# One hybrid decoder block on one core: block keys moved through DRAM scratch, gate projection from raw x in column groups, scores and probabilities half a unit later

## The chip, the cores and the metric

The kernel runs on one core of a Trainium2 chip. The metric is the device time of one execution in microseconds, as the median of several executions of the same program. A profiled execution gives the trace that is read here.

## What is computed

A sequence of 256 tokens with a width of 1024 goes through one decoder block, all in float32: an RMS norm, an input projection, a mixer with two groups of heads, an output projection, a SwiGLU feed-forward layer and a final norm.

```python
h = rms_norm(x, norm1_gain[l])
proj = h @ w_in[l]
gq, gk, gv, gr, g_low, mq, mk, mv = parts            # 256, 256, 512, 512, 16, 512, 512, 512 columns
log_a = log_sigmoid(g_low @ w_gate_up[l] + b_gate[l]) / 16
o_gla = rms_norm(gla_chunked(gq, gk, gv, log_a)) * silu(gr)
q_m, k_m = rotary(mq, positions), rotary(mk, positions)
o_moba = rms_norm(moba_attention(q_m, k_m, mv))       # 256 tokens are one block: causal softmax attention
x = x + concatenate([o_gla, o_moba]) @ w_out[l]
h = rms_norm(x, norm2_gain[l])
x = x + (silu(h @ w_ffn_gate[l]) * (h @ w_ffn_up[l])) @ w_ffn_down[l]
return rms_norm(x, final_norm_gain)
```

## The kernel before

All matrix products with weights are made from three float32r products: each operand is split into a high part (a rounded copy) and a low part (the rest), and hi x hi, hi x lo and lo x hi are added up in PSUM (`product`, L505 to L510). Attention, transposes and the small products take plain float32 operands, each of which shows in the trace as two matmul records.

The weights come in **units** of 128 x 2048 floats (1 MB). SyncE (SP) loads a unit with two DMAs into one of three raw buffers (`rows_unit`, L344; the DMAs have line L342), ScalarE (ACT) rounds it to `w_hi` (L877), VectorE (DVE) subtracts to get `w_lo` (L1137), and TensorE (PE) runs 24 matmuls of 512 columns over it (`in_unit`, L593). `w_hi` and `w_lo` have six buffers. Units 0 to 11 are the input projection, two for each block of 512 columns, in the order gate queries and keys, block queries (`mq`), block keys (`mk`), block values, gate values, `gr`; units 12 to 15 are the output projection; then eleven feed-forward phases follow with three units each. The load of unit u waits until the `lo` part of unit u - 3 is made (`raw_free`, L362).

Units 0 and 1 are special: they are loaded, split and multiplied row by row (128 x 512 pieces, `load_first` L330, `split_first` L903 and L1150, `first_row` L555) beside the transposes of x (L534) and the scaling of the transposed x by the norm gain (`take_xT`, L897 on ACT for the high part, L1144 on DVE for the low part).

The order of work on every engine is written out by hand, and each engine works in that order. SP is one queue of DMA issues too: what stands behind a wait there is issued late. On PE the small products stand between the two token halves of a unit (`midway`) or behind a unit (`after`):

```python
            midway = {2: [logits], 7: [moba_k_transposed], 8: [moba_scores],
                      9: [probs_transposed], 10: [moba_outputs, gla_updates], 11: [gla_outputs, lambda: heads_transposed(0, (3, 0))]}
            after = {3: [cumulate], 7: [gla_scores]}
```

What the change touches:

- `gate_low` (L580): the 16-column projection `g_low`. ACT copies the weights four times side by side as high part, GpSimd (POOL) makes the low part (L477), and 16 float32r matmuls of 256 columns (L589, L590) multiply them with the split, gain-scaled x.
- `rotate` (L1228) on DVE: rotary for `mq` (which 0) and `mk` (which 1), six operations each.
- The queries of the block attention are turned by one DVE transpose within 32 x 32 squares (L1257), written to DRAM (`squares_out`, L387) and read back as columns by four DMAs (`columns_back`, L392); ACT copies them to `mT_q` (L964). The keys are turned by PE (`moba_k_transposed`, L635) in the middle of unit 7 and copied out of PSUM by ACT (L960) and DVE (L1261) to `mT_k`.
- `moba_scores` (L654) in the middle of unit 8, the softmax on DVE (L1276 to L1286) and ACT (L973), `probs_transposed` (L670) in the middle of unit 9.
- Behind it: the squares of the heads on ACT (L986, L1007), their sums on DVE (L1298), the low part of the transposed heads (`take_headsT`, L1326, through L1141), and the output projection on PE, which starts when that low part is there.

## Time and profile before

| | |
|---|---|
| median of 3 executions | 302.33 us (301.77 to 302.42) |
| the profiled execution's own time | 301.75 us |
| its span in the trace | 300.0 us |
| PE busy | 292.4 us (97%), 1373 matmul records |
| DVE busy | 242.4 us (81%) |
| ACT busy | 171.6 us (57%) |
| POOL busy | 19.1 us (6%) |
| DMA | 55.45 MB, mean 185 GB/s |
| chain that ended last | PE 94%, DMA 2%, DVE 1%, issue 1%, POOL 1% |
| mean granted TensorE clock | 0.996 of full speed |

The busy time is the union of the instructions of an engine. The chain that ended last is followed back from the last instruction: at each step to what released it, or to the instruction before it on its engine. The own time of the execution is 1.75 us longer than its span.

### The profile page before, as it was taken

The page shows a single profiled execution, that of the slowest core. Times are in us where ns is not written, and L with a number is a line of the kernel's source. Part 1 is how long each engine was busy: PE and PEld are TensorE (multiplying, and loading weights), DVE is VectorE, ACT ScalarE, POOL GpSimd, SP SyncE. Part 2 cuts the span into 40 slices and gives each one's busy share as a digit, 9 for nine tenths or more (in the row PEclk, how much of TensorE's full clock was granted, in tenths as well). Part 3 has the DMA queues.
Part 4 walks back from the last instruction along what each step waited for, and adds up shares of the span by engine and source line. Part 5 has one row for each costly group of instructions (what it writes and reads, how often), then busy time and mean ns, then how long its engine had stood idle before and what let it go on. Part 6 is the DMA issues. An engine that isn't in the chain of part 4 may idle for free.

```text
span 300.0 us, 4026 instructions
## 1 busy us (share of the span) xinstructions
PE 292.4 (97%) x1373; PEld 243.3 (81%) x1373; DVE 242.4 (81%) x403; ACT 171.6 (57%) x242; POOL 19.1 (6%) x41
## 2 busy tenths in 40 slices
PE   7999999999999999999999999999999999999992
PEld 7788888788898888887888888888888888888881
DVE  1999999977879687988888888889897978787155
ACT  2898999969765897717170808080808080813123
POOL 5050100000021001300000000000000000000011
PEclk9999999999999999999999999999999999999998
DMA  7987836737867121392929292929291929030003
GB/s 235 364 289 266 263 119 251 218 131 264 298 190 227 53 92 70 95 329 90 331 82 336 79 343 69 346 66 352 63 363 47 367 54 366 25 120 0 0 0 140
DMA packets 37318, 55.45 MB, mean 185 GB/s; under 512 B 2950, under 2 KB 26554, under 8 KB 37306
## 3 DMA queue, kind: packets, MB, share of 16 engines
q1 hardware_dynamic: 37140, 55.13, 54.4%
q10 hardware_dynamic: 166, 0.17, 0.2%
q8 instruction: 7, 0.11, 0.2%
q14 instruction: 5, 0.04, 0.0%
HBM read 53.72 MB, written 1.57 MB: 184 GB/s over the span
## 4 chain that ended last, share of the span: by engine, by line
PE 94%; DMA 2%; DVE 1%; issue 1%; POOL 1%; ACT 0%; SPq 0%; POOLq 0%; DVEq 0%
PE acc L508 15%; PE acc L510 15%; PE acc L509 15%; PE aux L508 13%; PE aux L509 13%; PE aux L510 13%; DMA raw<-in_w_in 2%; PE aux L613 1%; PE acc L562 1%; PE acc L565 1%; PE acc L568 1%; PE aux L683 1%; DVE x_sb L1366 1%; PE aux L707 1%; PE aux L665 1%
## 5 line engine op out<-in xcount | busy, mean ns | idle before, releaser
L1137 DVE TENSOR_TENSOR w_lo<-raw,w_hi 128x2048 fp32r<-128x2048 f32 x47 | 105.6, 2286 | 14.5 <-ACT w_hi L877 14.4
L877 ACT CAST w_hi<-raw 128x2048 fp32r<-128x2048 f32 x47 | 87.9, 1908 | 4.4 <-DMA raw<-in_w_ffn_up 2.1
L508 PE MATMUL aux<-w_hi,aT_hi 128*128 128x512 f32 (+1 forms) x180 | 69.8, 388 | 0.0
L509 PE MATMUL aux<-w_lo,aT_hi 128*128 128x512 f32 (+1 forms) x180 | 69.7, 387 | 0.0
L510 PE MATMUL aux<-w_hi,aT_lo 128*128 128x512 f32 (+1 forms) x180 | 69.7, 387 | 0.0
L1432 DVE STREAM_TRANSPOSE reuse_c<-reuse_c 32x128 f32<-32x128 f32 x160 | 48.4, 303 | 2.4
L1080 ACT CAST pT_hi<-reuse_c 128x512 fp32r<-128x512 f32 x10 | 6.2, 621 | 72.9 <-DVE reuse_c L1432 72.9
L508 PE MATMUL acc<-w_hi,aT_hi 128*128 128x512 f32 x118 | 47.1, 399 | 0.0
L510 PE MATMUL acc<-w_hi,aT_lo 128*128 128x512 f32 x118 | 46.1, 390 | 0.0
L509 PE MATMUL acc<-w_lo,aT_hi 128*128 128x512 f32 x118 | 46.0, 390 | 0.0
L508 PEld LDWEIGHTS aux<-w_hi,aT_hi 128*128 128x128 f32 x180 | 33.8, 188 | 6.9
L510 PEld LDWEIGHTS aux<-w_hi,aT_lo 128*128 128x128 f32 x180 | 33.8, 188 | 6.9
L509 PEld LDWEIGHTS aux<-w_lo,aT_hi 128*128 128x128 f32 x180 | 33.8, 188 | 6.8
L508 PE MATMUL acc<-w_hi,pT_hi 128*128 128x512 f32 x80 | 31.3, 392 | 0.0
L510 PE MATMUL acc<-w_hi,pT_lo 128*128 128x512 f32 x80 | 31.2, 390 | 0.0
L509 PE MATMUL acc<-w_lo,pT_hi 128*128 128x512 f32 x80 | 31.2, 389 | 0.0
L510 PEld LDWEIGHTS acc<-w_hi,aT_lo 128*128 128x128 f32 x118 | 22.2, 188 | 4.8
L508 PEld LDWEIGHTS acc<-w_hi,aT_hi 128*128 128x128 f32 x118 | 22.2, 188 | 4.7 <-issue 0.2
L509 PEld LDWEIGHTS acc<-w_lo,aT_hi 128*128 128x128 f32 x118 | 22.2, 188 | 4.4
L1063 ACT ACTIVATE reuse_c<-aux,rstd 128x256 f32<-128x256 f32 x22 | 10.0, 471 | 19.1 <-PE aux L510 17.9
L508 PEld LDWEIGHTS acc<-w_hi,pT_hi 128*128 128x128 f32 x80 | 15.0, 188 | 3.4 <-issue 0.3
L510 PEld LDWEIGHTS acc<-w_hi,pT_lo 128*128 128x128 f32 x80 | 15.0, 188 | 3.2
(203 smaller groups left out, 285.0 us busy)
## 6 DMA issues: line engine op xcount, KB each, us to landing
raw<-in_w_ffn_gate SPq DMA_DIRECT2D x22, 512.0 KB, 4.3
raw<-in_w_ffn_up SPq DMA_DIRECT2D x22, 512.0 KB, 5.4
raw<-in_w_ffn_down SPq DMA_DIRECT2D x22, 512.0 KB, 6.0
raw<-in_w_in SPq DMA_DIRECT2D x20, 512.0 KB, 4.8
raw<-in_w_out SPq DMA_DIRECT2D x8, 512.0 KB, 4.3
raw<-in_w_in SPq DMA_DIRECT2D x8, 256.0 KB, 6.2
x_sb<-in_x SPq DMA_DIRECT2D x2, 512.0 KB, 3.7
m_moves<-reuse_c SPq DMA_DIRECT2D x1, 512.0 KB, 2.7
```

What stands on the lines that cost most here:

```text
L508: nc.tensor.matmul(dst, left_hi[:, k, tok], right_hi, start=first, stop=False)
L509: nc.tensor.matmul(dst, left_hi[:, k, tok], right_lo, start=False, stop=False)
L510: return nc.tensor.matmul(dst, left_lo[:, k, tok], right_hi, start=False, stop=last)
L562: nc.tensor.matmul(acc[:, t, :], aT_hi[:, k, toks[t]], right_hi, start=k == 0, stop=False)
L565: nc.tensor.matmul(acc[:, t, :], aT_hi[:, k, toks[t]], right_lo, start=False, stop=False)
L568: last = nc.tensor.matmul(acc[:, t, :], aT_lo[:, k, toks[t]], right_hi, start=False, stop=k == KC - 1)
L613: last = nc.tensor.transpose(aux[:, bank, n * P:(n + 1) * P], src, ident[:, :])
L877: nc.scalar.copy(w_hi[:, slot % RING, :], raw[:, slot % RAW, :]).then_inc(hi_ready, 1)
L1063: nc.scalar.activation(silu_g[:, t, :], aux[:, GATE_UP_BANKS[parity][t], 0:FF], ACT.Silu, scale=rstd[:, 1, t:t + 1]).then_inc(silu_ready, 1)
L1080: nc.scalar.copy(dst, src.rearrange("p (k s) -> p k s", k=2)).then_inc(hiddenT_hi_ready, 1)
L1137: nc.vector.tensor_tensor(w_lo[:, slot % RING, :], raw[:, slot % RAW, :], w_hi[:, slot % RING, :].bitcast(f32), ALU.subtract).then_inc(lo_ ...
L1432: last = nc.vector.transpose(cols[SQUARE * c:SQUARE * (c + 1), :, :, g, :], rows[SQUARE * g:SQUARE * (g + 1), :, :, c, :])
```

## The change

1. **First loads.** SP issues row 0 of the weights behind the two halves of x, then waits until the first half of x has landed before it issues rows 1 to 7. ACT sums the squares of the first half of x at its start. Unit 2 is split in two halves on ACT and DVE, each when its own DMA has landed, and DVE does it ahead of the casts of the rotary angles.
2. **One table set.** ACT preloads the set with both logarithm and exponential, and the preload between units 5 and 6 is gone.
3. **`gate_low`.** POOL scales the 16 weight columns by the norm gain (two copies side by side, 32 columns), ACT copies the transposed x as it is out of PSUM (four copies of 128 x 512), and PE runs 8 plain float32 matmuls of 256 columns whose left side is 32 columns wide; they go to four groups of 32 output partitions. `w_up` is laid out in four groups (four DMAs for two).
4. **`rotate`.** Five operations for six, the first one of double width, with two temporaries.
5. **Keys.** DVE turns them as it does the queries, after the scratch of the queries has been written (`m_moved_out`), since both use the same squares; SP writes them to DRAM and reads them back by four DMAs, behind the load of unit 11. The eight transposes on PE and the two copies out of PSUM are gone.
6. **Order.** `moba_scores` and `probs_transposed` move from the middle of units 8 and 9 to their end. DVE splits unit 10 ahead of the softmax, not behind it.

```diff
--- before.py
+++ after.py
...
@@ -158,9 +158,10 @@
...
         gate_bias = mv[:, 0, W - QK:W]
-        rot_tmp = mv[:, :, 0:HEADS * HALF].rearrange("p t (h d) -> p t h d", h=HEADS)
-        low_w = w_hi[:, RING - 1, 0:KC * P].rearrange("p (k r w n) -> p k r w n", k=KC, w=2, n=RANK)
+        rot_tmp = [mv[:, :, HEADS * HALF * n:HEADS * HALF * (n + 1)].rearrange("p t (h d) -> p t h d", h=HEADS) for n in range(2)]
+        low_w = reuse_d[:, 512:512 + KC * SQUARE].rearrange("p (k w n) -> p k w n", k=KC, n=RANK)
+        xT_raw = [half[:, :].rearrange("p (b n) -> p b n", b=2)[:, b, :] for half in (reuse_a, reuse_b) for b in range(2)]
...
-        mT_k = reuse_f[:, 1024:2048].rearrange("p (h s) -> p h s", h=HEADS)
+        k_columns = reuse_d[:, :].rearrange("p (c n i) -> p c n i", c=QUADS, i=SQUARE)
+        k_rows = reuse_e[:, 1024:2048].rearrange("p (n c i) -> p c n i", c=QUADS, i=SQUARE)
...
@@ -334,20 +340,22 @@
 
             for t in range(T):
                 sp.dma_start(x_sb[:, t, :], x[0, t * P:(t + 1) * P, :]).then_inc(x_loaded[t], 16)
-            for n in range(KC):
+            load_first(0)
+            sp.wait_ge(x_loaded[0], 16)
+            for n in range(1, KC):
                 load_first(n)
 
...
@@ -367,15 +375,14 @@
                     sp.wait_ge(lo_ready, u - RAW - EARLY + 1)
 
             sp.dma_start(low_raw[:, :, :], w_in[0, :, LOW:LOW + RANK].rearrange("(k p) n -> p k n", p=P)).then_inc(low_loaded, 16)
-            for u in range(EARLY, RAW):
-                rows_unit(u, w_in[0], (u % 2) * 4 * P, 4, BLOCKS[u // 2], 512)
+            rows_unit(EARLY, w_in[0], (EARLY % 2) * 4 * P, 4, BLOCKS[EARLY // 2], 512, half_loaded)
...
             sp.wait_ge(up_zeroed, 1)
-            for n in range(2):
-                sp.dma_start(w_up[n * RANK:(n + 1) * RANK, :], w_gate_up[0]).then_inc(up_loaded, 16)
+            for n in range(QUADS):
+                sp.dma_start(w_up[n * SQUARE:n * SQUARE + RANK, :], w_gate_up[0]).then_inc(up_loaded, 16)
...
@@ -395,7 +402,9 @@
             in_units(RAW, 11)
             squares_out(m_squares_ready, 1, m_moves, m_squares, m_moved_out)
             columns_back(m_moved_out, m_moves, m_columns, m_columns_back)
+            squares_out(k_squares_ready, 1, k_moves, m_squares, k_moved_out)
             in_units(11, IN_UNITS)
+            columns_back(k_moved_out, k_moves, k_columns, k_columns_back)
             for n in range(OUT_UNITS):
                 u = IN_UNITS + n
                 raw_free(u)
@@ -473,9 +482,11 @@
                 nc.gpsimd.tensor_tensor(rstd[:, norm, t:t + 1], ms[:, norm, t:t + 1], minus_half[:, 0:1],
                                         ALU.pow).then_inc(rstd_ready, 1)
 
-            pool.wait_ge(low_hi_ready, 1)
-            nc.gpsimd.tensor_tensor(low_w[:, :, :, 1, :], low_raw[:, :, :].unsqueeze(2).to_broadcast(LOW_COPIES),
-                                    low_w[:, :, :, 0, :].bitcast(f32), ALU.subtract).then_inc(low_lo_ready, 1)
+            pool.wait_ge(low_loaded, 16)
+            pool.wait_ge(gains_ready, 1)
+            nc.gpsimd.tensor_tensor(low_w, low_raw[:, :, :].unsqueeze(2).to_broadcast(LOW_COPIES),
+                                    gains[:, NORM1_ROW:NORM1_ROW + KC].unsqueeze(2).unsqueeze(3).to_broadcast(LOW_COPIES),
+                                    ALU.mult).then_inc(low_w_ready, 1)
...
@@ -580,14 +591,12 @@
             def gate_low():
 
 
-                pe.wait_ge(low_hi_ready, 1)
-                pe.wait_ge(low_lo_ready, 1)
-                pe.wait_ge(xT_hi_ready, KC)
-                pe.wait_ge(xT_lo_ready, KC)
+                pe.wait_ge(low_w_ready, 1)
+                pe.wait_ge(xT_raw_ready, KC // 2)
                 for k in range(KC):
-                    left = w_hi[:, RING - 1, k * P:(k + 1) * P]
-                    nc.tensor.matmul(aux[:, 2, 0:SEQ], left, aT_hi[:, k, :], start=k == 0, stop=False)
-                    last = nc.tensor.matmul(aux[:, 2, 0:SEQ], left, aT_lo[:, k, :], start=False, stop=k == KC - 1)
+                    group = slice(k % QUADS * SQUARE, (k % QUADS + 1) * SQUARE)
+                    last = nc.tensor.matmul(aux[group, 2, 0:SEQ], low_w[:, k, :, :].rearrange("p w n -> p (w n)"),
+                                            xT_raw[k // 2][:, k % 2 * SEQ:(k % 2 + 1) * SEQ], start=k < QUADS, stop=k >= QUADS)
                 last.then_inc(low_in_psum, 1)
...
@@ -631,12 +640,6 @@
                     nc.tensor.matmul(aux[:, 3, dst], tri[:, :], log_hi[:, cols], start=True, stop=False)
                     last = nc.tensor.matmul(aux[:, 3, dst], tri[:, :], log_lo[:, cols], start=False, stop=True)
                 last.then_inc(cum_in_psum, 1)
-            def moba_k_transposed():
-                pe.wait_ge(rotated, 2)
-                for n, bank in enumerate((3, 0)):
-                    transposes(bank, [m_rot[:, 1, t, h, :] for h in (2 * n, 2 * n + 1)
-                                      for t in range(T)]).then_inc(mT_in_psum, 1)
...
@@ -654,16 +657,16 @@
             def moba_scores():
 
                 pe.wait_ge(mT_q_ready, 1)
-                pe.wait_ge(mT_by_act, 1)
-                pe.wait_ge(mT_by_dve, 1)
+                pe.wait_ge(k_columns_back, 16 * QUADS)
                 pe.wait_ge(a_ready, 2)
+                keys = k_columns.rearrange("p g (t h) i -> p t h g i", t=T)
                 for h in range(HEADS):
-                    last = nc.tensor.matmul(aux[:, 1, h * P:(h + 1) * P], mT_q[:, 0, h, :], mT_k[:, h, 0:P],
+                    last = nc.tensor.matmul(aux[:, 1, h * P:(h + 1) * P], mT_q[:, 0, h, :], keys[:, 0, h],
...
                 last.then_inc(scores_in_psum, 1)
                 for h in range(HEADS):
                     last = nc.tensor.matmul(aux[:, 2 + h // 2, (h % 2) * SEQ:(h % 2 + 1) * SEQ], mT_q[:, 1, h, :],
-                                            mT_k[:, h, :], start=True, stop=True)
+                                            keys[:, :, h], start=True, stop=True)
                     if h % 2:
                         last.then_inc(scores_in_psum, 1)
...
@@ -785,9 +788,8 @@
...
-            midway = {2: [logits], 7: [moba_k_transposed], 8: [moba_scores],
-                      9: [probs_transposed], 10: [moba_outputs, gla_updates], 11: [gla_outputs, lambda: heads_transposed(0, (3, 0))]}
-            after = {3: [cumulate], 7: [gla_scores]}
+            midway = {2: [logits], 10: [moba_outputs, gla_updates], 11: [gla_outputs, lambda: heads_transposed(0, (3, 0))]}
+            after = {3: [cumulate], 7: [gla_scores], 8: [moba_scores], 9: [probs_transposed]}
...
@@ -866,7 +868,7 @@
...
-            nc.scalar.preload_act_table(ACT.Exp)
+            nc.scalar.preload_act_table_set("natural_log_exp_and_others")
...
@@ -906,27 +908,36 @@
                 nc.scalar.copy(w_hi[:, n // 4, cols], raw[:, n // 4, cols]).then_inc(first_hi_ready, 1)
...
+            act.wait_ge(x_loaded[0], 16)
+            sum_squares(0, 0)
             act.wait_ge(gains_ready, 1)
             take_xT((0, 1))
+            def copy_xT(pair):
+                act.wait_ge(xT_lo_ready, 2 * pair + 2)
+                nc.scalar.copy(xT_raw[pair], aux[:, pair, :]).then_inc(xT_raw_ready, 1)
             for n in range(1, KC):
                 split_first(n)
                 if n % 2:
                     take_xT((n + 1, n + 2) if n < KC - 1 else ())
-            act.wait_ge(low_loaded, 16)
-            nc.scalar.copy(low_w[:, :, :, 0, :], low_raw[:, :, :].unsqueeze(2).to_broadcast(LOW_COPIES)).then_inc(low_hi_ready, 1)
-            split(2)
-            for t in range(T):
-                sum_squares(0, t)
+                if n in (5, KC - 1):
+                    copy_xT((n - 5) // 2)
+            for h in range(2):
+                act.wait_ge(half_loaded[h], 16)
+                half = slice(h * UNIT // 2, (h + 1) * UNIT // 2)
+                nc.scalar.copy(w_hi[:, EARLY, half], raw[:, EARLY, half]).then_inc((half_hi_ready, hi_ready)[h], 1)
+            for pair in range(2, KC // 2):
+                copy_xT(pair)
+            sum_squares(0, 1)
             split(3)
+            act.wait_ge(low_in_psum, 1)
             take_block(0, gqk)
             split(4)
             act.wait_ge(logits_ready, 1)
             then(nc.scalar.activation(soft, log_a, ACT.Abs))
             then(nc.scalar.activation(soft, soft, ACT.Exp, scale=-1.0))
             nc.scalar.activation(soft, soft, ACT.Ln, bias=one[:, :]).then_inc(soft_ready, 1)
-            act.wait_ge(low_in_psum, 1)
             split(5)
-            nc.scalar.preload_act_table(ACT.Exp)
             split(6)
             act.wait_ge(cum_in_psum, 1)
             nc.scalar.activation(reuse_c[:, 0:512], aux[:, 2, :], ACT.Exp)
@@ -956,8 +967,6 @@
...
             act.wait_ge(rotated, 2)
-            act.wait_ge(mT_in_psum, 1)
-            nc.scalar.copy(mT_k[:, 0:2, :], aux[:, 3, :].rearrange("p (h s) -> p h s", h=2)).then_inc(mT_by_act, 1)
             split(9)
             take_block(3, mv)
...
@@ -1188,15 +1197,21 @@
...
             nearest_turns()
+            for h in range(2):
+                dve.wait_ge((half_hi_ready, hi_ready)[h], 1)
+                half = slice(h * UNIT // 2, (h + 1) * UNIT // 2)
+                last = nc.vector.tensor_tensor(w_lo[:, EARLY, half], raw[:, EARLY, half], w_hi[:, EARLY, half].bitcast(f32),
+                                               ALU.subtract)
+            last.then_inc(lo_ready, 1)
             then(nc.vector.tensor_copy(turns_hi, turns))
             then(nc.vector.tensor_tensor(turns_lo, turns, turns_hi.bitcast(f32), ALU.subtract))
-            split(2)
-            for part in two_pi_parts(5)[:2]:
-                take_off(turns_hi.bitcast(f32), part)
-                take_off(turns_lo, part)
+            take_off(turns_hi.bitcast(f32), two_pi_parts(5)[0])
+            take_off(turns_lo, two_pi_parts(5)[0])
             dve.wait_ge(low_in_psum, 1)
             nc.vector.tensor_copy(lowT[:, :], aux[:, 2, 0:SEQ]).then_inc(lowT_ready, 1)
+            take_off(turns_hi.bitcast(f32), two_pi_parts(5)[1])
+            take_off(turns_lo, two_pi_parts(5)[1])
...
@@ -1232,12 +1247,14 @@
...
-                nc.vector.tensor_tensor(out_a, a, cos, ALU.mult)
-                nc.vector.tensor_tensor(out_b, b, cos, ALU.mult)
-                then(nc.vector.tensor_tensor(rot_tmp, b, sin, ALU.mult))
-                then(nc.vector.tensor_tensor(out_a, out_a, rot_tmp, ALU.subtract))
-                then(nc.vector.tensor_tensor(rot_tmp, a, sin, ALU.mult))
-                nc.vector.tensor_tensor(out_b, out_b, rot_tmp, ALU.add).then_inc(rotated, 1)
+                both, out = (v.rearrange("p t h (w d) -> p t (h w) d", w=2) for v in (m_raw, m_rot[:, which]))
+                nc.vector.tensor_tensor(out, both, cos_t[:, :, :].unsqueeze(2).to_broadcast([P, T, 2 * HEADS, HALF]), ALU.mult)
+                nc.vector.tensor_tensor(rot_tmp[0], b, sin, ALU.mult).then_inc(turned, 1)
+                nc.vector.tensor_tensor(rot_tmp[1], a, sin, ALU.mult).then_inc(turned, 1)
+                dve.wait_ge(turned, 2 * which + 1)
+                nc.vector.tensor_tensor(out_a, out_a, rot_tmp[0], ALU.subtract)
+                dve.wait_ge(turned, 2 * which + 2)
+                nc.vector.tensor_tensor(out_b, out_b, rot_tmp[1], ALU.add).then_inc(rotated, 1)
...
@@ -1256,9 +1273,10 @@
             dve.wait_ge(rotated, 1)
             nc.vector.transpose(m_squares, m_rows).then_inc(m_squares_ready, 1)
             rotate(1)
+            dve.wait_ge(rotated, 2)
+            dve.wait_ge(m_moved_out, 16)
+            nc.vector.transpose(m_squares, k_rows).then_inc(k_squares_ready, 1)
             split(8)
-            dve.wait_ge(mT_in_psum, 2)
-            nc.vector.tensor_copy(mT_k[:, 2:4, :], aux[:, 0, :].rearrange("p (h s) -> p h s", h=2)).then_inc(mT_by_dve, 1)
             split(9)
...
                 last.then_inc(a_ready, 1)
+            split(10)
...
@@ -1285,7 +1304,6 @@
...
-            split(10)
             split(11)
             dve.wait_ge(probT_in_psum, 3)
```

**SP, around unit 11.** Before, the last two blocks of the queue (`reuse_a<-m_moves` reads the queries back):

```order
L387 DMA m_moves<-reuse_c 128x1024 [waits m_squares_ready]
L392 DMA reuse_a<-m_moves 32x4x256 [waits m_moved_out]
L392 DMA reuse_a<-m_moves 32x4x256 x3
L342 DMA raw<-in_w_in 128x2x512 [waits lo_ready]
L342 DMA raw<-in_w_in 128x2x512
L342 DMA raw<-in_w_out 128x1024 [waits lo_ready]
```

And in the changed kernel:

```order
L394 DMA m_moves<-reuse_c 128x1024 [waits m_squares_ready]
L399 DMA reuse_a<-m_moves 32x4x256 [waits m_moved_out]
L399 DMA reuse_a<-m_moves 32x4x256 x3
L394 DMA k_moves<-reuse_c 128x1024 [waits k_squares_ready]
L350 DMA raw<-in_w_in 128x2x512 [waits lo_ready]
L350 DMA raw<-in_w_in 128x2x512
L399 DMA reuse_d<-k_moves 32x4x256 [waits k_moved_out]
L399 DMA reuse_d<-k_moves 32x4x256 x3
L350 DMA raw<-in_w_out 128x1024 [waits lo_ready]
```

Five DMAs for the keys came in, one ahead of the load of unit 11 and four behind it and ahead of unit 12.

**DVE, from the second rotary to the softmax.** Before:

```order
L1240 TENSOR_TENSOR reuse_e<-reuse_e,mv 128x8x64 [waits dve_seq]
L1137 TENSOR_TENSOR w_lo<-raw,w_hi 128x2048 [waits hi_ready]
L1261 COPY reuse_f<-aux 128x512 [waits mT_in_psum]
L1137 TENSOR_TENSOR w_lo<-raw,w_hi 128x2048 [waits hi_ready]
L1270 COPY_PREDICATED reuse_b<-gla_mask,aux 128x2x128 [waits a_in_psum,consts_built,a_zeroed]
...
L1276 TENSOR_TENSOR reuse_e<-aux,causal 128x512 [waits scores_in_psum]
```

And in the changed kernel:

```order
L1257 TENSOR_TENSOR reuse_e<-reuse_e,mv 128x8x64 [waits turned]
L1278 STREAM_TRANSPOSE reuse_c<-reuse_e 128x1024 [waits m_moved_out,rotated]
L1146 TENSOR_TENSOR w_lo<-raw,w_hi 128x2048 [waits hi_ready] x2
L1288 COPY_PREDICATED reuse_b<-gla_mask,aux 128x2x128 [waits a_in_psum,consts_built,a_zeroed]
...
L1146 TENSOR_TENSOR w_lo<-raw,w_hi 128x2048 [waits hi_ready]
L1295 TENSOR_TENSOR reuse_e<-aux,causal 128x512 [waits scores_in_psum]
```

The transpose of the keys stands ahead of the splits of units 8 and 9, the copy out of PSUM between them is gone, and the split of unit 10 stands ahead of the softmax.

## Rows read from the trace of the kernel before

**Rows 1.** The page's part 1: busy time of each engine.
```profile
PE 292.4 (97%) x1373; PEld 243.3 (81%) x1373; DVE 242.4 (81%) x403; ACT 171.6 (57%) x242; POOL 19.1 (6%) x41
```
**Rows 2.** Waits of PE, whole span: us in total, times, longest.
```profile
PE acc L562 <- DVE w_hi L1156: 0.4, 1, 0.4
```
**Rows 3.** The chain that ended last: start us, us, what.
```profile
1.71 5.34 DMA raw<-in_w_in
7.07 0.44 DVE w_hi L1156
7.64 0.70 PE acc L562 x2
...
9.47 0.46 PE acc L562 x2
...
53.08 0.98 PE aux L613 x8
...
56.82 1.09 PE aux L650 x16
...
60.86 0.89 PE aux L661 x8
...
78.44 0.59 PE aux L695 x8
```
**Rows 4.** Timeline of ACT: start us, us, line, operation, idle before.
```profile
6.31 0.84 ACT L900 ACTIVATE aT_hi<-aux,gains 128x256 fp32r<-128x256 f32 x2 [3.04 <-PE aux L534]
8.00 0.62 ACT L906 CAST w_hi<-raw 128x512 fp32r<-128x512 f32 x1 [0.85 <-DMA raw<-in_w_in]
...
15.52 1.91 ACT L877 CAST w_hi<-raw 128x2048 fp32r<-128x2048 f32 x1 [1.07 <-DMA raw<-in_w_in]
...
27.21 1.28 ACT L926 ACT_TABLE_LOAD   x1
...
53.74 0.59 ACT L960 COPY reuse_f<-aux 128x512 f32<-128x512 f32 x1 [0.70 <-PE aux L613]
...
83.37 1.91 ACT L877 CAST w_hi<-raw 128x2048 fp32r<-128x2048 f32 x1 [2.07 <-DMA raw<-in_w_ffn_up]
```
**Rows 5.** Landing times: tile x_sb, then L332 (first rows), then L342 at 40:64.
```profile
DMA to landing us min/median/max: 3.3/3.7/4.2
...
DMA to landing us min/median/max: 5.3/6.2/6.7
...
DMA to landing us min/median/max: 3.4/4.5/6.3
```
**Rows 6.** Timeline of PE.
```profile
18.86 0.28 PE L589 MATMUL aux<-aT_hi,w_hi 128*128 128x256 f32 x1
...
20.86 0.22 PE L577 MATMUL aux<-ident,reuse_d 10*128 10x10 f32 x1
...
90.84 0.39 PE L508 MATMUL acc<-w_hi,aT_hi 128*128 128x512 f32 x1
```
**Rows 7.** Timeline of DVE.
```profile
47.55 1.25 DVE L1257 STREAM_TRANSPOSE reuse_c<-reuse_e 128x1024 f32<-128x1024 f32 x1
...
52.83 2.28 DVE L1137 TENSOR_TENSOR w_lo<-raw,w_hi 128x2048 fp32r<-128x2048 f32 x1
...
88.04 1.22 DVE L1298 TENSOR_REDUCE ss_h<-reuse_c 128x8 f32<-128x1024 f32 x1 [0.74 <-ACT reuse_c L1007]
...
89.38 1.41 DVE L1141 SCALAR_TENSOR_TENSOR aT_lo<-aux,gains,aT_hi 128x512 fp32r<-128x512 f32 x2
```
**Rows 8.** The page's part 6: KB each, median us to landing.
```profile
m_moves<-reuse_c SPq DMA_DIRECT2D x1, 512.0 KB, 2.7
```
**Rows 9.** Timeline of SP's queue: unit 11, unit 16.
```profile
55.58 0.47 SPq L342 DMA_DIRECT2D raw<-in_w_in  x1
...
77.92 0.38 SPq L342 DMA_DIRECT2D raw<-in_w_ffn_gate  x1
```
**Rows 10.** One stretch: us, busy of each engine, PEclk, DMA share, GB/s.
```profile
59.00:60.00 1.00, 1.00 (x6) 0.81 (x5) 0.95 (x3) 1.00 (x1) 0.00 (x0) 1.00 1.18 303
```

More of the change, by code:

```diff
@@ L227, in build_block @@
         gain_f_loaded = sem("gain_f_loaded")
+        half_loaded = [sem(f"half_loaded_{h}") for h in range(2)]
+        half_hi_ready = sem("half_hi_ready")
         raw_loaded = [sem(f"raw_loaded_{s}") for s in range(RAW)]
@@ L336, in _, with load_unit, rows_unit @@
                 sp.dma_start(x_sb[:, t, :], x[0, t * P:(t + 1) * P, :]).then_inc(x_loaded[t], 16)
[L337 removed]
+            load_first(0)
+            sp.wait_ge(x_loaded[0], 16)
+            for n in range(1, KC):
                 load_first(n)
[L340 to L344 removed]
+            def load_unit(slot, parts, sems=None):
+                for (dst, src), loaded in zip(parts, sems or (raw_loaded[slot],) * 2):
+                    sp.dma_start(dst, src).then_inc(loaded, 16)
+            def rows_unit(slot, w, row, n_rows, col, width, sems=None):
                 buf = raw[:, slot, :].rearrange("p (k n) -> p k n", k=n_rows)
@@ L349, in rows_unit @@
                                   w[row + h * half * P:row + (h + 1) * half * P, col:col + width]
-                                  .rearrange("(k p) n -> p k n", p=P)) for h in range(2)])
+                                  .rearrange("(k p) n -> p k n", p=P)) for h in range(2)], sems)
             def gate_up_unit(slot, j, h):
```

24 lines of the change are left out of this document (11 added, 13 removed).

## Prediction, before any run of the change

> **What bounds the kernel now.** I read the busy times first: PE is busy for 292.4 of 300.0 us, every other engine for less than 243 [rows 1]. Then the waits of PE: beside its warm-up, the only one in the whole span is 0.4 us before the first real matmul [rows 2]. Then the chain that ended last: x and row 0 of the weights land, DVE rounds row 0 at 7.07, PE starts at 7.64 and is the chain to the end [rows 3], but for a tail of some 11 us that the change does not touch. So the time is the start of PE, plus its work, plus waits, of which there are none today. A change can gain only by an earlier start or by less work on PE, and it keeps the gain only if what PE waits for comes earlier by as much. That second half is where I look for losses. One matmul of 512 columns takes 0.23 us here (0.46 for two [rows 3]), a unit of 24 takes 5.5. "The same" is within 0.2%, 0.6 us, about what a measurement of this kernel can tell from no change.
>
> **Start.** Row 0 lands at 7.05, 5.34 after its issue, in one queue with x before it and seven rows behind it [rows 3]. Those behind it now leave after the first half of x has landed. PE needs two things for its first product: the rounded row 0, and the first scaled column of x, which ACT makes from 6.31 to about 6.75 [rows 4]. PE itself waits 0.4 there [rows 2], so at most 0.4 is to be had. Below: nothing, or a loss. The issue of row 1 moves from about 2.2 (an issue takes 0.47 [rows 9]) to about 4.6 (x lands 3.3 to 4.2 after its issue [rows 5]). Landing takes 3.3 in an empty queue and 5.3 behind others [rows 5], so row 1 is there at 7.9 to 9.9, against 8.00 before [rows 4]; PE wants it at about 9.1 with 0.6 for ACT's cast, so the loss is 0 to 1.4. I take a gain of 0.3: fewer transfers beside row 0, and rows that still come faster than the 1.37 us that PE spends on one. ACT's sum of squares of the first half lies in its idle time before 6.31 (3.04 us [rows 4]).
>
> **gate_low.** From 18.86 to 20.86 PE runs 16 float32r matmuls of 256 columns, 2.0 us [rows 6]. Now it runs 8 plain ones. Plain float32 of 128 columns takes 0.22 (0.89 for four [rows 3]), so 256 columns take 0.44 and eight in sequence 3.5: 1.5 more than before. But they go to four groups of output columns. The trace has two such pairs: four matmuls 64 columns wide took 0.59 where four full ones took 0.89, and eight that use half of the rows took 1.09, 0.14 each, for 0.22 [rows 3]. Two groups thus gave a factor of 1.5 to 1.6. With four groups I take twice that, 3, so 1.2 us and a gain of 0.8. Bounds: the ideal factor of 4 gives 0.9 us, a gain of 1.1; none gives a loss of 1.5. The Trainium skill (TensorE: Matmul & The Clock Gate, Part 3) has 2.38 for three column tiles, which by its proportion is an estimate of 3.2 for four; by that gate_low would take 1.1 us and the sum would be 0.1 lower. The 64-wide row agrees in kind. The skill (TensorEngine Tiling (Array Packing), Key Properties) also says that changing the tiling mode drains TensorE; no row before shows what a drain costs by itself.
>
> What gate_low waits for: ACT casts unit 2 in halves and then copies the last two pieces of x. ACT's copy of 128 x 512 out of PSUM takes 0.59 [rows 4], two of the four lie after unit 2. That unit had landed at 15.52 and was done at 17.4 [rows 4]; in halves the first is cast before the second is there, and it ends about 17.0. That makes 18.1, and PE comes at 18.86 - 0.3 = 18.6. Covered, by half a microsecond. ACT gives up one cast for it, and has two table loads less, 1.28 each [rows 4]; none of these is on the path now, they only move the exponentials and with them the rotary on DVE forward. The extra `w_up` DMAs hide as the old ones did.
>
> **Keys.** Eight transposes leave PE: 0.98 [rows 3], 1.0 with the restart. The strided keys that the scores now read, and the moved places of scores and probabilities, change nothing in PE's work: as many interruptions as before. So PE has 0.3 + 0.8 + 1.0 = 2.1 us less by the end of unit 8.
>
> DVE pays 1.25 for the transpose of the keys, ahead of the split of unit 8 [rows 7], and gets back about 0.15 from each shorter rotary. The split of unit 8 ended at 52.83 + 2.28 = 55.1; alone this makes 56.0. PE begins unit 8 at 56.82 + 1.09 = 57.9 before [rows 3], now at 55.8. I expect the earlier exponentials to move DVE forward by 0.5 to 1, which leaves no wait there, and the load of unit 11, which waits for this split, where it was. The scratch of the queries is written in 2.7 us [rows 8], from 47.55 + 1.25 on; DVE spends the time from there to 52.83 on the second rotary [rows 7], so that new wait is covered too.
>
> **Where the gain is given back, 1: the columns.** On SP the four read-backs of the keys stand behind unit 11, whose second DMA goes out at 55.58 [rows 9] and lands 4.5 later (3.4 to 6.3 [rows 5]), at 60.1. Half a megabyte at 303 GB/s [rows 10] takes 1.7: 61.8. PE is ready for the scores at 57.9 + 5.5 - 2.1 = 61.3. I count a wait of 0.4. Bounds: the read-backs are issued by about 57.7; with the 3.4 of the fastest neighbour there is no wait, and with the 6.3 of the slowest they land at 64.0, a wait of 2.7.
>
> **Where it is given back, 2: the heads.** Scores began at 60.86; now at 61.7, because they stand half a unit later. The softmax, ACT's splits of units 12 and 13 behind it, and the low part of unit 13 on DVE follow; that low part frees the buffer of unit 16, issued at 77.92 [rows 9]. ACT idles 2.07 for that load and splits it from 83.37 [rows 4]. These move later by about 0.6 (a wait for unit 9 inside falls away). Behind them ACT makes two squares. The second ended at 88.0 before because it waited for PE; now ACT's own row gives 84.0 + 1.8 + 0.6 + 0.5 + 0.6 = 87.5. DVE's sum, and the low part of the first heads (88.04 to 90.1 [rows 7]: 2.1 us), end at 89.6. PE wants that at 90.84 [rows 6] - 2.1 + 0.4 = 89.1. A second wait of 0.5. Bounds 0 and 1.2 (all of the 0.85 by which scores are later, and 0.3 for the loads).
>
> **The sum.** -0.3 - 0.8 - 1.0 + 0.4 + 0.5 = -1.2. Behind the heads the work on ACT and DVE is tied to the same row at 88.04, which comes 0.5 earlier, and had some 0.9 to spare against PE. So I see no third loss at a gain of 1.2. The profiled execution's own 301.75 becomes 300.5; it was the fastest of those shown, and against their median of 302.33 the forecast is 301.1.
>
> **The rivals.**
>
> *A, the gain is kept.* Columns land by 61.3 and the heads are in time: -2.1, with the best start and the ideal factor -2.5. For it: the wait of ACT for unit 16 may shrink, as unit 13 is loaded sooner when DVE splits unit 10 before the softmax. Against it: the chain above was counted from rows, and it gives back half. 300.2, range 299.8 to 300.6.
>
> *B, the column groups do not overlap.* gate_low takes 3.5 for 2.0, with a drain perhaps more. -0.3 + 1.5 - 1.0 = +0.2 of PE's work; PE comes too late to wait for columns, but the heads hang on the scores and still cost their 0.5. +0.7: 303.0, range 302.4 to 303.4. Against it: the 0.59 for four 64-wide matmuls.
>
> *C, slower: the keys' way through DRAM.* One mechanism in one place: PE stands before the scores because `k_columns_back` comes late. With the landing at 64.0 of the slowest neighbour it waits 2.7; softmax, heads and splits hang on the scores, so nothing of it is won back, and the heads' 0.5 comes on top: -2.1 + 2.7 + 0.5 = +1.1, 303.4. It decides from a landing at 62.9 on, where the sum is zero. A late split of unit 8 pushes unit 11 and the columns behind it by as much. For it: SP, DVE and DMA all lie in this path, and the PE transposes that it replaces were done in 1 us. Against it: the queries' scratch took 2.7 in the same queue, and the counted landing is a microsecond short of the point.
>
> *D, part of it does not act.* Row 0 lands as before, or a row comes late and eats the start's gain, and the heads take their full 1.2: -0.4 in all, 301.9.
>
> **Chances.** Forecast 0.54, own range 300.6 to 301.6; A 0.16; B 0.09; C 0.10; D 0.11. Faster by over 0.2% is under 301.7: 0.54 + 0.16, 0.70. Slower by over 0.2% is over 302.9: C and half of B, 0.15. The rest, D and half of B, is the same, 0.15. The range leaves out 2 in 10: a third of A, half of B and C. That makes 300.0 to 302.9.
>
> **What would show it.** PE's first matmul at 7.2 to 7.5. The eight matmuls of gate_low in 0.9 to 1.4 us, and 8 transposes missing at 53. In PE's waits two new rows: one before the scores with the DMA of the read-back as releaser, 0 to 1, and one before the first matmul of the output projection with DVE's L1141 row as releaser, 0 to 1. The load of unit 16 issued at about 78.5. Wrong would be: a wait of PE before a first row over 0.5; a wait at gate_low (ACT late with its copies); a wait at unit 8 for `w_lo`; or any wait after 92.

## The result, and the profile after

The changed kernel takes 303.71 us, median of 11 runs (302.34 to 305.77), against 302.06 for the kernel before (11 runs on the same chip). The ratio is 1.0063, with a 95% interval of 1.0045 to 1.0082: slower by 1.65 us. Forecast were 301.1 (1.2 less than the 302.33 then known) and a range of 300.0 to 302.9: the time went up where it was to go down, and lies outside the range.

The eleven executions fall into two groups. Seven have a mean granted clock of 0.994 to 0.997 and lie at 302.34 to 303.80 (median 303.25); four have 0.988 to 0.990 and lie at 304.77 to 305.77. The profiled execution is one of the four (305.58, span 303.6), so it shows all of the loss and about 2 us that most executions don't have.

The busy times, part 1 of the page, answer to [rows 1]:

```profile
PE 293.7 (97%) x1365; PEld 243.1 (80%) x1365; DVE 241.9 (80%) x402; ACT 169.6 (56%) x243; POOL 17.1 (6%) x41
```

PE has 8 records less and 1.3 us more of busy time. The 8 are the eight transposes of the keys: a transpose shows as one record, not as two like the other plain float32 products. The waits of PE (total, times, longest), beside [rows 2]:

```profile
PE aux L664 <- issue: 2.3, 1, 2.3
PE acc L536 <- DVE w_lo L1170: 1.2, 1, 1.2
PE aux L710 <- DVE state L1336: 0.3, 1, 0.3
PE acc L519 <- issue: 0.2, 1, 0.2
```

L536 is the warm-up, the same as before. The wait of 0.4 before the first row is gone, but this trace gives no credit for it to the change: PE was still busy with the transposes of x when row 0 was ready (experiment 7, with the start as it was, has no such wait either). Three are new: 2.3 ahead of the scores (L664), 0.3 ahead of the GLA outputs (L710), 0.2 at the output projection. "issue" names no releaser; what it waits for is `k_columns_back`, as the queue and the experiments below show. The chain that ended last (start, us, what) has it in place:

```profile
8.34 0.66 PE acc L573 x2
...
19.43 1.00 PE aux L598 x16
...
56.39 0.43 PE acc L519
...
62.06 2.31 issue
64.37 1.64 PE aux L664 x8
66.01 2.89 PE aux L668 x8
...
94.37 0.47 PE acc L519
```

Beside [rows 3, 6]: the first row is 0.7 later, gate_low (L598) takes 1.00 for 2.00, and unit 8 begins at 56.39, 1.5 earlier than 57.91. So far the change is ahead. Then PE stands for 2.31, and the scores take 1.64 + 2.89, 4.5 in all. Before, the first tile's four heads took 0.89 [rows 3] and the second tile's

```profile
61.75 1.73 PE aux L665 x8
```

so 2.6 in all. The output projection comes at 94.37, 3.5 later than the 90.84 of [rows 6]. How the scores came to be slow stands in the table of stretches of the changed kernel (us; busy PE, PEld, DVE, ACT, POOL; PEclk; DMA share; GB/s):

```profile
62.10:64.30 2.20, 0.00 (x0) 0.00 (x0) 0.00 (x0) 1.77 (x1) 0.00 (x0) 1.00 1.08 278
64.40:64.90 0.50, 0.50 (x4) 0.50 (x5) 0.00 (x0) 0.00 (x0) 0.00 (x0) 0.92 1.03 410
64.90:68.50 3.60, 3.60 (x13) 3.12 (x12) 2.24 (x4) 0.80 (x5) 0.00 (x0) 0.54 0.97 388
68.50:70.00 1.50, 1.50 (x8) 1.23 (x7) 1.03 (x2) 0.85 (x5) 0.00 (x0) 1.00 0.02 5
```

After PE had stood, the granted clock went to its lower level (1.2 GHz, 0.54 as the mean of that stretch) for some 3.6 us, and came back before 68.5. The queue of SP in the same stretch (start, us, line, transfer):

```profile
53.93 0.34 SPq L394 DMA_DIRECT2D k_moves<-reuse_c  x1
56.11 0.91 SPq L350 DMA_DIRECT2D raw<-in_w_in  x2
57.44 1.77 SPq L399 DMA_DIRECT2D reuse_d<-k_moves  x4
59.26 3.38 SPq L350 DMA_DIRECT2D raw<-in_w_out  x4
```

Unit 11 leaves at 56.11, the four read-backs of the keys from 57.44 to 58.8. They land 5.2 us after their issue in the median and 5.5 at most, the last at about 64.3.

### The profile page after: what moved, and what is told of

Its sections match the earlier page's. It is cut to its first block, busy times and chain, and to the rows that moved or that the text cites. A ratio compares the mean times of both kernels' runs of the same rounds, so it can differ in the third digit from the quotient of the medians.

```text
span 303.6 us, 4012 instructions
## 1 busy us (share of the span) xinstructions
PE 293.7 (97%) x1365; PEld 243.1 (80%) x1365; DVE 241.9 (80%) x402; ACT 169.6 (56%) x243; POOL 17.1 (6%) x41
## 4 chain that ended last, share of the span: by engine, by line
PE 91%; DVE 3%; issue 2%; ACT 2%; POOL 1%; POOLq 0%; DVEq 0%; ACTq 0%
PE acc L519 14%; PE acc L521 13%; PE acc L520 13%; PE aux L521 13%; PE aux L520 13%; PE aux L519 13%; PE acc L536 1%; PE acc L573 1%; ACT w_hi L879 1%; PE acc L576 1%; PE acc L579 1%; PE aux L668 1%; DVE w_lo L1146 1%; PE aux L622 1%; PE aux L545 1%
## 5 line engine op out<-in xcount | busy, mean ns | idle before, releaser
L1146 DVE TENSOR_TENSOR w_lo<-raw,w_hi 128x2048 fp32r<-128x2048 f32 x46 | 103.2, 2284 | 14.5 <-ACT w_hi L879 14.4
L879 ACT CAST w_hi<-raw 128x2048 fp32r<-128x2048 f32 x46 | 85.9, 1909 | 8.9 <-DMA raw<-in_w_in 5.5
```

Source lines behind the costliest of these rows:

```text
L879: nc.scalar.copy(w_hi[:, slot % RING, :], raw[:, slot % RAW, :]).then_inc(hi_ready, 1)
L1146: nc.vector.tensor_tensor(w_lo[:, slot % RING, :], raw[:, slot % RAW, :], w_hi[:, slot % RING, :].bitcast(f32), ALU.subtract).then_inc(lo_ ...
```

## The experiments

All were timed against the kernel before on their own chip; its median was 302.06 to 302.13 in every batch, so the medians below can be set side by side. The theory: the key columns land late, because of unit 11 ahead of them in the queue; PE stands, and in some executions it also loses its clock. Rivals: the start is at fault, or the place of scores and probabilities half a unit on.

**1. Columns ahead of unit 11.**

```diff
+            columns_back(k_moved_out, k_moves, k_columns, k_columns_back)
             in_units(11, IN_UNITS)
-            columns_back(k_moved_out, k_moves, k_columns, k_columns_back)
```

> The changed kernel with the four loads of the key columns issued ahead of the load of unit 11. Theory 1, the key columns are late because they queue behind unit 11: they are issued at about 57.0 us instead of 57.4 to 58.8 and, with no unit in front of them, land 4 us or less later, by 61.5; PE's wait ahead of the scores falls from 2.31 us to 0.3 or less, the scores take 2.6 us again instead of 4.5, and the time falls by 2.0 to 2.5 us from the 303.7 of the changed kernel, to 301.2 to 301.7. Rival, the late first loads: unit 11 is now later still (landing about 65 us), ACT's and DVE's splits slide, a new PE wait comes after unit 10, and the time stays at 303 or more. Rival, the order half a unit on costs by itself: the scores start on time and the heads still wait, time 302.5 or more.

Measured: 302.16 us (12 runs, ratio 1.0008, 0.9993 to 1.0023), 1.55 less than the change. The columns left at 57.31 and landed 3.0 after their issue in the median, 3.2 at most. The waits of PE behind its warm-up:

```profile
PE aux L710 <- DVE state L1336: 0.8, 1, 0.8
PE aux L622 <- ACT reuse_e L982: 0.2, 1, 0.2
```

None ahead of the scores, and none of the twelve executions lost its clock (means 0.994 and more). This is the largest part of the loss. It fell short of the 301.7 that was expected: part of it came back as 0.8 and 0.2 behind the scores, since ACT now casts unit 11 at 64.97 and only then gets to the softmax.

**2. The columns one load further back.** The suspected cost doubled:

```diff
+                if n == 0:
+                    columns_back(k_moved_out, k_moves, k_columns, k_columns_back)
```

(inside the loop that loads the `w_out` units, and not ahead of it).

> The changed kernel with the key columns one place further back on SP's queue, behind the load of unit 12 (two pieces of 512 KB); the suspected cost doubled. Theory 1: unit 12 is issued at about 57.4 to 58.4 us, the columns from 59 us, they land at 66 to 68 us, the wait ahead of the scores is 4 to 6 us in place of 2.31, and the time 305 to 308. Rival, the place on the queue matters little, since the transfers share the engines anyway: 303.7 to 304.2.

Measured: 309.75 us (6 runs, 1.0252, 1.0222 to 1.0283), more than the highest figure expected. The largest wait of PE, then stretches of the same kernel:

```profile
PE aux L665 <- issue: 6.0, 1, 6.0
```

```profile
64.00:65.00 1.00, 0.00 (x0) 0.00 (x0) 0.00 (x0) 0.00 (x0) 0.00 (x0) 1.00 1.11 263
...
66.00:67.00 1.00, 0.00 (x0) 0.00 (x0) 0.00 (x0) 0.00 (x0) 0.00 (x0) 0.50 1.08 243
...
71.00:72.00 1.00, 1.00 (x4) 0.75 (x3) 0.93 (x3) 0.00 (x0) 0.00 (x0) 0.50 0.00 0
```

The wait was in the range that was expected. What had been left out is that all six executions now lose the clock (means 0.980 to 0.988): it is at its lower level already while PE stands, and still there at 71 to 72, when the scores run. With no load, one and two ahead of the columns the kernel takes 302.16, 303.71 and 309.75 us, and the columns land 3.0, 5.2 and 6.0 us after issue in the median.

**3. and 4. PE kept at work while it waits.**

```diff
                 pe.wait_ge(mT_q_ready, 1)
+                for n in range(WARM):
+                    nc.tensor.matmul(aux[:, 0, 0:P], mT_q[:, n % 2, n // 2 % HEADS, :],
+                                     mT_q[:, n % 2, n // 2 % HEADS, :], start=True, stop=True)
                 pe.wait_ge(k_columns_back, 16 * QUADS)
```

With 20 of them:

> The changed kernel with 20 extra matmuls (128x128, float32, into a bank that nobody reads) on PE ahead of its wait for the key columns; nothing else moves. They take about 20 x 0.11 = 2.2 us by the first eight scores of the kernel before. Theory 1: they fill the 2.3 us in which PE stood, so the scores start at about the same 64.4 us; what follows them runs at a granted clock of 1.00, scores 2.6 us instead of 4.5, and the runs at 305 us, which the changed kernel shows beside those at 303, go: median 303.0 to 303.3. Rival, the scores are slow because the transfers crowd what they read, not by the clock: they still take about 4.5 us and the median stays at 303.7.

Measured: 305.40 us (4 runs, 1.0108, 1.0093 to 1.0123). My price for one matmul was half of the true one (the row of [rows 3] is four heads in 0.89, not eight), so they overshot the wait. The chain:

```profile
62.05 4.46 PE aux L662 x40
66.51 0.91 PE aux L667 x8
```

What it does show: the first four heads take 0.91 again, not 1.64. The transfers beside them ended while the scores ran, though (410 GB/s from 66 to 67, 82 from 67 to 68), so this run alone doesn't tell the clock from the traffic. With 10:

> The changed kernel with 10 extra matmuls (128x128, float32, nobody reads them) on PE ahead of its wait for the key columns. In the run with 20 of them each took 0.22 us (4.46 us in all), so 10 take 2.2 us and end at about the time at which the columns land. Theory 1, the idle PE loses its clock: scores 2.6 us at a granted clock of 1.00 in all executions, none at 305 us, median 303.0 to 303.4 against 303.71. Rival, the clock falls for another reason than the wait: some executions still lie at 305 us and the median stays at 303.7.

Measured: 304.00 us (6 runs, 303.17 to 304.90; 1.0066, 1.0045 to 1.0087). Timeline of PE:

```profile
61.53 2.39 PE L662 MATMUL aux<-reuse_f 128*128 128x128 f32 x20
65.20 1.16 PE L667 MATMUL aux<-reuse_d,reuse_f 128*128 128x128 f32 x8 [1.27 <-DMA reuse_d<-k_moves]
66.19 1.89 PE L671 MATMUL aux<-reuse_d,reuse_f 128*128 128x256 f32 x8
```

Here the trace names the releaser, the read-back. The scores took 2.5 (65.20 to 67.73), beside as much traffic as the slow ones had, which were at 388 GB/s:

```profile
66.00:67.00 1.00, 1.00 (x8) 0.92 (x7) 0.61 (x1) 0.00 (x0) 0.00 (x0) 1.00 1.03 410
67.00:68.00 1.00, 1.00 (x7) 0.87 (x6) 0.93 (x4) 0.00 (x0) 0.00 (x0) 1.00 1.04 414
```

So it isn't DMA traffic that made them slow; the granted clock is 1.00 here. All six executions have a mean clock of 0.994 or more, and so have the four with 20 matmuls: filling the gap keeps the clock, as far as ten executions can tell when 4 of 11 had lost it. The median did not fall to the 303.0 to 303.4 that I expected, though. It lies 0.75 above the 303.25 of the changed kernel's seven executions that kept their clock. In the profiled execution the columns landed 0.8 later than in that of the change; whether the dummy work has a part in that stays open.

**5. The keys by PE again**, scores and probabilities where the change has them.

```diff
-            squares_out(k_squares_ready, 1, k_moves, m_squares, k_moved_out)
-            columns_back(k_moved_out, k_moves, k_columns, k_columns_back)
...
-            midway = {2: [logits], 10: [moba_outputs, gla_updates], ...
+            midway = {2: [logits], 7: [moba_k_transposed], 10: [moba_outputs, gla_updates], ...
```

> The changed kernel with the keys turned by PE as before (eight transposes in the middle of unit 7, copied by ACT and DVE), no key squares and no key columns; scores and probabilities stay half a unit on. Theory 1: no wait ahead of the scores, 1.0 us of transposes more, 303.7 - 2.3 - (the clock's part) + 1.0 = 301.6 to 302.3. Rival, the later order itself costs: waits of PE behind the scores (before the outputs and the output projection) remain above 0.5 us together and the time stays at 302.8 or more.

Measured: 301.96 us (12 runs, 0.9996, 0.9988 to 1.0005). PE's waits behind its warm-up:

```profile
PE aux L712 <- DVE state L1339: 0.3, 1, 0.3
PE acc L515 <- issue: 0.3, 1, 0.3
```

So even with the columns first in the queue (302.16) the way through DRAM was not better than eight transposes on PE; the 0.2 between the two is within their intervals.

**6. Scores and probabilities back in the middle of units 8 and 9**, on top of that.

```diff
-            midway = {2: [logits], 7: [moba_k_transposed], 10: ...
-            after = {3: [cumulate], 7: [gla_scores], 8: [moba_scores], 9: [probs_transposed]}
+            midway = {2: [logits], 7: [moba_k_transposed], 8: [moba_scores], 9: [probs_transposed], 10: ...
+            after = {3: [cumulate], 7: [gla_scores]}
```

(and DVE's split of unit 10 behind the softmax again).

> The changed kernel with the keys turned by PE and with scores and probabilities in the middle of units 8 and 9, as before: what is left of the change is the start, the gate's low rank product, the one table set and the rotation. Theory 1: 301.96 of the kernel with the keys by PE, less the 0.6 us that PE still waits there around the head outputs (0.3 and 0.3): 301.3 to 301.7. Rival, the half unit on was a gain (no wait of PE ahead of the scores): here PE waits for the key copies in unit 8, and the time is 302.1 or more.

Measured: 301.24 us (7 runs, 0.9971, 0.9960 to 0.9982), just below what was expected, and faster than the kernel before. PE waits nowhere behind its warm-up. The half unit costs 0.72.

**7. The half unit alone, on the kernel before.** The same lines moved the other way, DVE's split of unit 10 among them.

> The kernel before with one edit: scores and probabilities after units 8 and 9 instead of in their middle, with DVE's split of unit 10 ahead of the scores. Theory 1: the keys are there, so no wait ahead of the scores; the heads come 2.7 us later and PE waits 0.3 to 0.8 us around the head outputs and the output projection: 302.3 to 302.9. Rival, the order costs nothing: 302.1. Rival, the order is the cause of most of the loss: 303.3 or more.

Measured: 302.95 us (8 runs, 1.0031, 1.0019 to 1.0043), +0.8, just above what was expected. The wait that it brings:

```profile
PE aux L707 <- DVE state L1317: 0.3, 1, 0.3
```

Two kernels give the same price for the same move, 0.7 and 0.8. It doesn't need late keys.

**8. and 9. The start.** First all of it undone:

```diff
             load_first(0)
-            sp.wait_ge(x_loaded[0], 16)
...
-            act.wait_ge(x_loaded[0], 16)
-            sum_squares(0, 0)
             act.wait_ge(gains_ready, 1)
```

> The changed kernel with the start as before: SP issues all of the first loads without waiting for the first half of x, and ACT squares x only after the first rows. Theory 1: the first matmul of the first rows moves from 8.34 us back to about 7.6 us, but the key columns come no earlier than the queue lets them, so the wait ahead of the scores grows by as much or by a part: 303.1 to 303.7. Rival, the late start is the cause of the loss: time 302.5 or less, and the wait ahead of the scores smaller than 1.5 us, because all of the later loads are issued earlier.

Measured: 302.57 us (11 runs, 1.0016, 1.0007 to 1.0026), 1.14 less than the change, near to what the rival had said and not the theory. Then SP's wait alone:

> The changed kernel with one line less at the start: SP issues the first loads 1 to 7 without waiting for the first half of x; ACT still squares that half early. Theory 1: SP's wait is what holds the later loads, unit 3 among them, and by it DVE's chain up to the key transpose (1.3 us in the kernel with the whole start undone): the wait ahead of the scores is 1.4 us or less and the time 302.5 to 302.8. Rival, ACT's early squares are what delays: time 303.4 or more, wait 2.0 us or more.

Measured: 302.54 us (12 runs, 1.0023, 1.0011 to 1.0035). So SP's wait accounts for all of it. The wait ahead of the scores is 1.0 here, in place of 2.3:

```profile
PE aux L662 <- issue: 1.0, 1, 1.0
```

The queue and ACT of this kernel:

```profile
12.30 0.94 SPq L348 DMA_DIRECT2D raw<-in_w_in  x2
...
52.46 0.43 SPq L392 DMA_DIRECT2D k_moves<-reuse_c  x1
```

```profile
19.14 1.90 ACT L877 CAST w_hi<-raw 128x2048 fp32r<-128x2048 f32 x1 [0.44 <-DMA raw<-in_w_in]
```

And of the changed one:

```profile
13.38 0.94 SPq L350 DMA_DIRECT2D raw<-in_w_in  x2
```

```profile
21.71 1.91 ACT L879 CAST w_hi<-raw 128x2048 fp32r<-128x2048 f32 x1 [2.44 <-DMA raw<-in_w_in]
```

Unit 3 is issued 1.1 later in the changed kernel and cast 2.6 later, DVE splits it 1.7 later (23.72 and 22.00), and from there DVE is busy for all but 0.5 of 29 us up to the key transpose. The keys go to scratch at 53.93 and not at 52.46. An issue that was held for x in the third microsecond thus pays at the 64th. The other traces bear this out, with some spread: ACT stands 1.2 to 2.5 us for unit 3 in all seven that have SP's wait, and at most 0.4 in the five that have the rest of the change without it. In neither of the two kernels of 8 and 9 did an execution lose its clock (means 0.994 and more, with a wait of 1.4 and 1.0 in the profiled ones).

A part of the 1.14 is therefore the clock. Against the 303.25 of the executions that kept it, the start costs 0.7 in the changed kernel.

**10. Columns first, and the start as before.**

> Both edits on the changed kernel: the key columns issued ahead of unit 11, and the start as before. Theory 1 (the columns land late, in part because of unit 11 in front of them and in part because the later first loads hold DVE's chain up to the key transpose by 1.3 us): both parts go, PE does not wait ahead of the scores at all, unit 11 lands 1.2 us earlier than with the first edit alone, and the time is 301.2 to 301.7, below the kernel before. Rival, only the queue position matters: the same 302.16 as with the first edit alone. Rival, the wait moves to what unit 11 feeds: PE waits 0.8 us or more behind unit 10 and the time is 302 or more.

Measured: 301.51 us (12 runs, 0.9986, 0.9974 to 0.9998), faster than before by a narrow margin, and 0.65 below experiment 1. The first theory had the time. There is no wait ahead of the scores, but 0.7 ahead of the GLA outputs, nearly the wait of the last rival, without the 302 that it gave.

**11. The states ahead of unit 14's split** on DVE, in the kernel of 10.

```diff
             split(13)
-            split(14)
...
                 nc.vector.tensor_copy(dst, src).then_inc(states_ready, 1)
+            split(14)
             dve.wait_ge(rstd_h_ready, 1)
```

> The kernel with the key columns ahead of unit 11 and the start as before, and one more edit: DVE reduces the squares of the MoBA heads and copies the states before its split of unit 14 instead of behind it. There PE waited 0.68 us for the state copy, and 0.2 us more stood around it. Theory: that wait is what the order half a unit on costs, so it goes and the time is 300.6 to 301.0, level with or below the 300.84 of the kernel with the keys by PE in the middle of unit 7. Rival, unit 14's split comes 2.4 us later, holds back the load that reuses its buffer, and PE waits ahead of the output projection or the first gate and up unit instead: 301.5 or more.

Measured: 302.13 us (12 runs, 1.0004, 0.9988 to 1.0020), 0.6 worse than without it. The wait moved instead of going:

```profile
PE acc L517 <- issue: 1.0, 1, 1.0
```

It is now at the output projection (at 90.75). The rival was right on the time and on the place, but its way isn't what the trace shows. The load that reuses unit 14's buffer did go out later, at 84.72 for 81.08, and PE waited nowhere for it. What PE waited for is the low part of the first heads, which DVE began at 89.91, for 89.08 without the edit. Ahead of that DVE stood 0.36 for ACT's squares, and ACT had cast unit 16 before them at 85.08 for 84.22; that load waits for unit 13, which the edit doesn't touch. How much of the 0.6 is the edit's own stays open.

**12. The best version: keys by PE, scores and probabilities in the middle, start as before.** What is left of the change is gate_low with its four DMAs of `w_up`, the one table set, unit 2 in halves and the shorter rotary.

> The kernel above (keys by PE, scores and probabilities in the middle of their units) with the start as before too. What is left of the change is the product of 1.0 us in place of 2.0 at the end of the first rows, the table set and the rotation. Theory 1: 1.0 us below the kernel before, 301.0 to 301.4. Rival, the gate's product gives nothing, since a later wait takes it back: 302.0.

Measured: 300.84 us (5 runs, 300.46 to 301.24; ratio 0.9958, 0.9945 to 0.9971), 1.3 below the kernel before, a little more than expected, and 2.9 below the change. Its gate_low on PE's timeline, two pieces:

```profile
19.49 0.64 PE L592 MATMUL aux<-reuse_a,reuse_d 128*32 128x256 f32 x8
19.94 0.61 PE L592 MATMUL aux<-reuse_b,reuse_d 128*32 128x256 f32 x8
20.49 0.23 PE L582 MATMUL aux<-ident,reuse_d 10*128 10x10 f32 x1
```

From 19.49 to 20.49, 1.0 us. The other 0.3 of the gain wasn't taken apart.

The medians, from the kernel before to the changed one:

| step | us | difference |
|---|---|---|
| kernel before | 302.1 | |
| gate_low, table set, unit 2 in halves, rotary | 300.84 | -1.3 |
| + the start | 301.24 | +0.4 |
| + scores and probabilities half a unit on | 301.96 | +0.7 |
| + keys through DRAM, columns first (PE has 1.0 less to do) | 302.16 | +0.2 |
| + columns behind unit 11 | 303.71 | +1.55 |

The intervals of the kernels behind the +0.4 and the +0.2 overlap. That the start costs something rests on three pairs of one sign: this 0.4, the 0.65 of experiments 1 and 10, and the 1.14 in the changed kernel, 0.7 with the clock kept.

## Why the prediction was wrong

**Start, -0.3: wrong in sign.** It cost 0.4 where PE waits for nothing behind it, 0.65 with the columns first, and 1.14 in the changed kernel, 0.7 without the clock. The gain that was counted exists: in experiment 5 row 0 is rounded at 6.32 for 7.07, and PE starts at 7.19 for 7.64 without a wait. But it shows only where PE's transposes of x are done by then, in one of the seven traces with this start. The step that failed is "I take a gain of 0.3: ... rows that still come faster": I followed the delay of the issue only as far as the first rows, and costed nothing for the loads behind them in the same queue, unit 3 first.

**gate_low, -0.8: right, and better.** 1.00 for 2.00. Against the 3.5 estimated for eight such matmuls in sequence that is a factor of 3.5. The chain shows no gap ahead of them (the row before starts at 18.98, takes 0.45, and they start at 19.43), so no time for a drain is seen there. The Trainium skill (TensorE: Matmul & The Clock Gate, Part 3) has 2.38 for three column tiles, by which I had estimated 3.2 for four; this trace is a little above it. Rival B is out.

**Keys, -1.0 on PE: right.** From unit 2 to the GLA scores PE takes 34.7 (20.52 to 55.23) where it took 35.7 (21.02 to 56.75).

**The columns, +0.4: this is the term that failed most.** The step read "Half a megabyte at 303 GB/s [rows 10] takes 1.7: 61.8". It treated the read-backs as one block that starts when unit 11 has landed. In fact they are four issues of 0.44 each from 57.44 on, with unit 11 ahead of them (issued 56.11 to 57.02) and unit 12 behind (from 59.26), and the last lands at 64.3, where PE stood for 2.31 and not for 0.4. My own upper bound, the slowest neighbour's 6.3 and 64.0, was passed by 0.3; I took the low end because it could be worked out, and the rows did not say that it was the nearer. Rival C was the case that came: it had this mechanism and this place, 2.7 for the wait (2.31 in the profile) and 303.4 for the time (303.71). That the time came so near is in part luck: against the kernel before it had +1.1 where +1.65 was measured, since it kept the gain of the start and knew nothing of the clock, and it was set on a median of 302.33 that proved to be 302.06. It got a chance of 0.10 since "the queries' scratch took 2.7 in the same queue" spoke against it; but the last load ahead of that one had been issued 4 us earlier. The Trainium skill (DMA: Bandwidth & Descriptors, Two DMAs through the same engine are not ordered) says that within one queue of one engine descriptors start in order. The 3.0, 5.2 and 6.0 us with no load, one and two ahead agree with that.

**The clock: not in any case.** The wait was priced at its length. In 4 of 11 executions it cost about 2 us more; in the profiled one that is the 1.64 + 2.89 of the scores against 2.6.

**The heads, +0.5: right in size, half right in place.** 0.7 and 0.8 by two experiments. PE's wait of 0.3 at the output projection (experiment 5) is where I had it; the other, 0.3 for the state copy, which stands behind two splits on DVE, had been left out. Experiments 5 to 7 show that the move costs this much without late keys. With the keys through DRAM it can't simply be taken back: even in experiment 1 the last column landed at about 61.8, while the middle of unit 8, which begins at 56.1 there, is at about 59.

The steps of the table add up to the +1.65 because they lead from one kernel to the other; that is no further proof of them. Their sizes by cause are: -1.3 for what was kept in experiment 12, +0.4 for the start, +0.7 for the half unit, +0.2 for the keys' way with the columns first, +1.55 for unit 11 ahead of them, in which the clock's part lies. "What would show it" named the wait with the read-back as releaser, but gave it 0 to 1.

## What to carry to other kernels

A transfer that PE waits for is priced by its place in the queue: count what lies ahead of it and what is issued beside it, and take the landing of a neighbour that had the same company, not of one that stood alone. A step that is moved off a full engine gains only if its result still comes before it is needed; here 1.0 us on PE was traded for 11.7 us from the key transpose to landed columns. And a wait put into an issuing queue is followed down that queue to the end: one at the third microsecond delayed the 64th.

## What the runs showed of the hardware

In the profiled execution of the changed kernel a stand of PE of 2.3 us was followed by the lower level of its clock for 3.6 us, and the scores took 4.5 for 2.6. By their mean clocks, 4 of 11 executions of this kernel lost it. Of the kernels whose profiled execution has a stand of 1.0 or 1.4 us none of 23 executions lost it; of the one with 6.0 all six did. How long PE stood in the executions without a profile isn't known, nor what sets the four apart from the seven. A gap in PE's work thus can have two prices, its length and the slow work after it.

The start of PE varies by more than the start's edit. The eight transposes of the first half of x took 1.04 us in two of the profiled executions (the kernel before, and the one of experiment 5) and 1.21 to 1.91 in the twelve others, with the granted clock shown as 1.00 in all. The changed start gave a first row at 7.19 and at 8.28, the old start one at 7.64 and (experiment 7) at 8.56. A difference of 0.7 in the first row of two profiles therefore says nothing of an edit, which only the medians of many runs could price here.
